# A mixing stage rewritten: four stacked S5 taps, attention in the transposed layout, another order of weights and joins

## The reference, cut to what matters

```python
for l in range(2):
    x = layer_norm(a * x + 0.5 * swiglu(x, ...), ...)      # d_ff 2816
    x = layer_norm(a * x + hybrid_mix(x, ...), ...)
    x = layer_norm(a * x + memory_cross_attention(x, mem, ...), ...)
    x = layer_norm(a * x + 0.5 * swiglu(x, ...), ...)

def hybrid_mix(x):
    dq, dk, dv, mq, mk, mv, mo, mi, mf, su = split_columns(x @ w_in, IN_WIDTHS)
    # differential attention: 4 heads, two maps of width 64 each, values of width 128
    dq, dk = apply_rope(dq), apply_rope(dk)
    s = where(k_chunk <= q_chunk, q k^T / 8, -inf)         # per head and map
    a_out = rms_norm((softmax(s1) - lam * softmax(s2)) @ dv) * (1 - lambda_init)
    # mLSTM: 4 heads of width 64, a causal convolution of 4 taps and silu ahead of it
    mq, mk = silu(causal_conv([mq, mk]))
    h = mlstm_chunkwise(q, k, v, ig, log_sigmoid(f))
    b_out = sigmoid(mo) * rms_norm(h)
    # S5: 16 groups of 16 channels, each driving a complex diagonal state of 64
    states = scan(lam_bar, b_bar @ u);  y = gelu(real(c @ states) + d * u)
    c_out = y * sigmoid(y @ glu_w + glu_b)
    return concat([a_out, b_out, c_out]) @ w_out
```

## Time and profile before

| | us |
|---|---|
| runs | 1377.54, 1377.72, 1380.18; median 1377.72 |
| the profiled execution | 1376.7, span 1374.9, mean granted clock 0.959 |
| PE busy | 1264.1 (92%), 6568 products |
| DVE busy | 812.4 (59%) |
| ACT busy | 578.1 (42%) |
| POOL busy | 192.8 (14%) |
| `mix` of layer 0, x turned to last product | 223.4 to 417 |
| `mix` of layer 1, x turned to last product | 912 to 1089 |

### The profile page before, as it was taken

The page is one execution under the profiler, slowest core; times in us unless marked ns, Lnnn a source line. Parts: engine busy times, 40 slices in busy tenths (PEclk is TensorE's granted clock), DMA queues, the critical chain, the costliest instruction groups (busy, mean ns, idle before and its releaser), DMA issues.

```text
span 1374.9 us, 15895 instructions
## 1 busy us (share of the span) xinstructions
PE 1264.1 (92%) x6568; PEld 1068.6 (78%) x6568; DVE 812.4 (59%) x1130; ACT 578.1 (42%) x656; POOL 192.8 (14%) x181
## 2 busy tenths in 40 slices
PE   6999999989669999999999999999875999799997
PEld 5788888878558888888887888888754887688885
DVE  5578556593675556444566785465937736544454
ACT  4444444425433535444443444444263335444441
POOL 1018000372000000000010180003720000000000
PEclk9999999999789999999999999999976999899999
DMA  8655555433024365555547555544211434455551
GB/s 282 236 184 184 184 184 163 144 123 123 31 92 158 128 204 184 184 188 192 192 148 270 186 184 184 184 151 156 92 61 62 139 118 143 152 184 186 190 193 43
DMA packets 155911, 219.52 MB, mean 160 GB/s; under 512 B 6816, under 2 KB 127776, under 8 KB 155840
## 3 DMA queue, kind: packets, MB, share of 16 engines
q1 hardware_dynamic: 152448, 205.61, 44.9%
q0 software_dynamic: 3120, 11.85, 2.4%
q10 hardware_dynamic: 272, 1.05, 0.2%
HBM read 217.44 MB, written 1.05 MB: 159 GB/s over the span
## 4 chain that ended last, share of the span: by engine, by line
PE 65%; issue 16%; DVE 11%; ACT 3%; POOL 2%; DMA 1%; SPq 0%; DVEq 0%; POOLq 0%
PE PS L469 20%; PE PS L470 19%; PE PS L471 19%; DVE WL L1376 3%; ACT WH L1043 1%; PE PS L500 1%; DMA RAW<-in_ffn_w_up 1%; DVE COUT L1560 1%; DVE ZS L1548 1%; PE PS L964 1%; PE PS L988 1%; ACT XH L1043 1%; PE PS L537 1%; POOL RO L1997 1%; ACT PR L1160 1%
## 5 line engine op out<-in xcount | busy, mean ns | idle before, releaser
L1376 DVE TENSOR_TENSOR WL<-RAW,WH 128x2048 fp32r<-128x2048 f32 (+1 forms) x198 | 445.3, 2253 | 272.4 <-ACT WH L1043 272.3
L1043 ACT ACTIVATE WH<-RAW 128x2048 fp32r<-128x2048 f32 (+1 forms) x198 | 370.5, 1877 | 148.4 <-DMA RAW<-in_ffn_w_up 128.5
L469 PE MATMUL PS<-WH,XH 128*128 128x512 f32 x832 | 333.4, 401 | 24.6 <-DVE WL L1376 9.4
L470 PE MATMUL PS<-WL,XH 128*128 128x512 f32 x832 | 327.5, 394 | 0.0
L471 PE MATMUL PS<-WH,XL 128*128 128x512 f32 x832 | 327.0, 393 | 0.0
L469 PEld LDWEIGHTS PS<-WH,XH 128*128 128x128 f32 x832 | 158.2, 190 | 59.0 <-DVE WL L1376 9.9
L471 PEld LDWEIGHTS PS<-WH,XL 128*128 128x128 f32 x832 | 158.2, 190 | 33.8
L470 PEld LDWEIGHTS PS<-WL,XH 128*128 128x128 f32 x832 | 158.4, 190 | 31.0
L469 PE MATMUL PS<-WH,HH 128*128 128x512 f32 x352 | 138.6, 394 | 5.7 <-issue 5.7
L470 PE MATMUL PS<-WL,HH 128*128 128x512 f32 x352 | 137.6, 391 | 0.0
L471 PE MATMUL PS<-WH,HL 128*128 128x512 f32 x352 | 137.6, 391 | 0.0
(11 more groups left out here) (312 smaller groups left out, 1805.5 us busy)
## 6 DMA issues: line engine op xcount, KB each, us to landing
RAW<-in_ffn_w_gate SPq DMA_DIRECT2D x88, 512.0 KB, 3.7
RAW<-in_ffn_w_up SPq DMA_DIRECT2D x88, 512.0 KB, 4.7
RAW<-in_ffn_w_down SPq DMA_DIRECT2D x88, 512.0 KB, 4.3
RAW<-in_w_in SPq DMA_DIRECT2D x44, 512.0 KB, 4.4
RAW<-in_xattn_wkv SPq DMA_DIRECT2D x32, 512.0 KB, 4.1
RAW<-in_xattn_wq SPq DMA_DIRECT2D x16, 512.0 KB, 4.4
RAW<-in_w_out SPq DMA_DIRECT2D x12, 512.0 KB, 4.0
RAW<-in_xattn_wo SPq DMA_DIRECT2D x12, 512.0 KB, 4.0
```

Source lines behind the costliest of these rows:

```text
L469: nc.tensor.matmul(out_ap, sh, mh, start=first, stop=False)
L470: nc.tensor.matmul(out_ap, sh, ml, start=False, stop=False)
L1043: return nc.scalar.activation(dst, src, ACT.Copy)
L1376: return v.tensor_tensor(dst, full, hi.bitcast(F32), ALU.subtract)
```

## The change

Only `mix`, its preparation in FFN0, the order of its weights and the constants are touched. `xattn`, the FFN products and the boundaries' own work are as before.

- S5 goes by four taps (TAPS = 4, 64 steps). `s5_gather` stacks u by taps on the partitions with 16 products by slices of the identity into one bank, ScalarE copies it to U4. `s5_in` is 16 products with K = 128 and N = 64 (before: 32 with K = 32, N = 128). The states are two batches on VectorE, the turning back included (`s5_states`). `s5_local` is 8 products, `s5_out` 16 with M = 128 (before: 32 with M = 32), `s5_scatter` 16 products that undo the gather, and a copy.
- In FFN0: three `s5_turn` instead of one, `s5_taps` in two parts with N = 128 instead of 64, 12 copies to PB and 8 to KM on ScalarE instead of one and four, `skip_taps` 8 operations instead of 2, one more DMA on GpSimd's queue, KM cleared by GpSimd in each layer.
- DQ and DK are taken in column form, so they come out transposed; `turn_q` and its copies are gone. The rotary turn is on VectorE, in that layout, with TensorE swapping the halves (`swap_halves`, 4 products with N = 512). GpSimd's `rope` and `turn_back` are gone.
- The masks of the diff heads are added by TensorE in PSUM; the maximum and the exponential read PSUM; the row sums come from a column of ones in DV (N = 129), both maps are transposed (6 instead of 3) and multiplied (6 instead of 3), and divided at evacuation.
- Decay: TensorE adds the triangle in `spread`, ScalarE's exponential has the bias; `decay_args` is gone. The first conv tap is on ScalarE, straight from PSUM. Two Newton-like root chains of VectorE are one `pow` each on GpSimd.
- Order: the projections are DV, DQ0, DK0, SU, MQ, MK, DQ1, DK1, MM. The mid units are mid 0, mid 1, W0, W1, mid 2, W2, mid 3, W3, W4. The splits of W3 and W4 stand ahead of the last head, the second join (W3) is taken tile by tile, with the last `turn_cat` between its tiles.

The diff, cut to its core:

```diff
-PAIRS = TILES // 2
-STEPS = SEQ // 2
+BANDS = TILES // 2
+TAPS = 4
+STEPS = SEQ // TAPS
...
-        order += [(l, "DQ", 0), (l, "DQ", 1), (l, "SU", 0), (l, "MQ", 0), (l, "MK", 0), (l, "DK", 0), (l, "DK", 1),
-                  (l, "DV", 0), (l, "DV", 1), (l, "MM", 0), (l, "MM", 1)]
-        order += FILL["mid", l]
-        order += [(l, "W", i) for i in range(5)]
+        order += [(l, "DV", 0), (l, "DV", 1), (l, "DQ", 0), (l, "DK", 0), (l, "SU", 0), (l, "MQ", 0), (l, "MK", 0),
+                  (l, "DQ", 1), (l, "DK", 1), (l, "MM", 0), (l, "MM", 1)]
+        mid = FILL["mid", l]
+        order += mid[0:2] + [(l, "W", 0), (l, "W", 1)] + mid[2:3] + [(l, "W", 2)] + mid[3:4] + [(l, "W", 3), (l, "W", 4)]
...
+            def s5_gather(l):
+                pe.wait_ge(ut_ready.sem, ut_ready.at(l, 1))
+                for tap in range(TAPS):
+                    r = 32 * tap
+                    out_ap = PS[r:r + 32, 5, :].rearrange("p (f j k) -> p j f k", f=2, j=BANDS)
+                    for j in range(BANDS):
+                        mm = nc.tensor.matmul(out_ap[:, j], ident[:, 32 * j:32 * j + 32],
+                                              UT[:, :, tap * STEPS:tap * STEPS + STEPS], start=True, stop=True)
...
+            def diff_scores(l, h):
+                b = head_bank(h)
...
+                for q0, q1, k1 in ((0, P, P), (P, SEQ, SEQ)):
+                    for m in range(2):
+                        r = 64 * m
+                        nc.tensor.matmul(PS[:, b + m, q0:q0 + k1], DQT[r:r + 64, u, h % 2, q0:q1],
+                                         DKT[r:r + 64, u, h % 2, 0:k1], start=True, stop=False,
+                                         skip_group_check=True)
+                        mm = nc.tensor.matmul(PS[:, b + m, q0 + k1 - 64:q0 + k1], kst[r:r + 1, K_EARLY:K_EARLY + P],
+                                              kst[r:r + 1, K_FAR:K_FAR + 64], start=False, stop=True,
+                                              skip_group_check=True)
...
+            def spread(l):
+                pe.wait_ge(cols_read.sem, cols_read.at(l, 1))
+                for i in range(2):
+                    for hh in range(2):
+                        h = 2 * i + hh
+                        pick = ident[0:4, h:h + 1].to_broadcast([4, P])
+                        nc.tensor.matmul(PS[:, i, hh * SEQ:hh * SEQ + SEQ], pick, R_MAX, start=True, stop=False, ...)
+                        nc.tensor.matmul(PS[:, i, hh * SEQ:hh * SEQ + P], ident, tri, start=False, stop=True, ...)
+                        nc.tensor.matmul(PS[:, 3, h * P:h * P + P], pick, R_MAX[:, P:SEQ], start=True, stop=False)
+                        mm = nc.tensor.matmul(PS[:, 3, h * P:h * P + P], ident, tri, start=False, stop=True)
...
+                pe.wait_ge(conv_done.sem, conv_done.at(l, 4))
+                unit_ready(UNIT[l, "MM", 0])
+                form_a_tile(UNIT[l, "MM", 0], 0, 0, XH, XL, 0)
+                swap_halves(l, 3)
+                form_a_tile(UNIT[l, "MM", 0], 0, 0, XH, XL, 1).then_inc(unit_used.sem, 1)
+                diff_scores(l, 1)
+                diff_scores(l, 2)
+                cols(l)
+                s5_scatter(l)
...
+                mid(l, 1, 3)
+                mlstm_scores(l, 0)
+                mlstm_scores(l, 1)
+                diff_out(l, 2)
+                diff_scores(l, 3)
+                mlstm_scores(l, 2)
+                mlstm_scores(l, 3)
+                fill_read("mid", l, 1)
                 mlstm_num(l)
...
                 rows_product(w, [6], CH, CL, True, False)
                 rows_product(w + 1, [7], CH, CL, False, False)
-
+                diff_turn(l, 3)
+                pe.wait_ge(do_read.sem, do_read.at(l, 3))
+                mid(l, 2, 6)
+                diff_out(l, 3)
                 pe.wait_ge(b_ready.sem, b_ready.at(l, 1))
...
+                turn_cat(l, CATM, 0, 7)
+                pe.wait_ge(a_ready.sem, a_ready.at(l, 1))
+                fill_read("mid", l, 2)
+                turn_cat(l, CATA, 0, 6)
...
+                mid(l, 3, 7)
                 pe.wait_ge(cat_lo.sem, cat_lo.at(l, 2))
-                unit_ready(w + 3)
-                rows_tile(w + 3, [0, 1], CH, CL, 0, False, False)
+                unit_ready(w3)
+                rows_tile(w3, [0, 1], CH, CL, 0, False, False)
                 pe.wait_ge(a_ready.sem, a_ready.at(l, 2))
-                turn_cat(l, 2, 2, 5)
+                turn_cat(l, CATA, 2, 4)
```

VectorE's list in the new `mix`, up to the mLSTM:

```diff
+                diff_max(l, 0)
+                s5_states(l, 0)
                 gates_in(l)
+                s5_states(l, 1)
                 split()
                 conv(l, 0)
-                split()
-                s5_turn_in(l, 0)
...
+                mid_split(l, 0)
+                rope(l, 2)
+                gates_out(l)
+                conv(l, 1)
...
+                mid_split(l, 3)
+                diff_sums(l, 2)
+                diff_combine(l, 2)
+                decay_scores(l, 2)
+                decay_scores(l, 3)
```

More of the change, by code:

```diff
@@ L422, in load_ffn, with load_fill @@
                 load_down(l, s, FFN_UNITS - 1, BLOCKS - 1)
-            def load_fill(where, l):
-                for kl, kind, i in FILL[where, l]:
+            def load_fill(where, l, first=0, last=None):
+                for kl, kind, i in FILL[where, l][first:last]:
                     load_cols(UNIT[kl, kind, i], wkv_v, kl, 256 * i + (D if kind == "V" else 0))
@@ L577, in ffn @@
                     rows_product(b + 4 + 3 * j, [0, 1], HH, HL, False, False)
[L578 to L581 removed]
+                    if s == 0 and 5 <= j <= 7:
+                        s5_turn(l, j - 5)
+                    if s == 0 and j == 8:
+                        s5_taps(l, 0)
                 j = BLOCKS - 2
@@ L694, in s5_local, with s5_in @@
+            def s5_in(l):
+                pe.wait_ge(u4_ready.sem, u4_ready.at(l, 1))
+                for i in range(TILES):
+                    for part in range(2):
+                        o = part * 256 + (i % 4) * STEPS
+                        mm = nc.tensor.matmul(PS[:, 4 + i // 4, o:o + STEPS], PB[:, i, part, :], U4[:, i, :],
+                                              start=True, stop=True)
+                    if i % 4 == 3:
+                        mm.then_inc(bu_done.sem, 1)
             def s5_local(l):
@@ new lines, in s5_scatter @@
+            def s5_scatter(l):
+                pe.wait_ge(gelu_done.sem, gelu_done.at(l, 1))
+                g = U4[:, :, :].rearrange("p (f j) k -> p j f k", f=2)
+                for j in range(BANDS):
+                    out_ap = PS[32 * j:32 * j + 32, 2, :].rearrange("p (f a k) -> p a f k", f=2, a=TAPS)
+                    for tap in range(TAPS):
+                        mm = nc.tensor.matmul(out_ap[:, tap], ident[:, 32 * tap:32 * tap + 32], g[:, j],
+                                              start=True, stop=True)
+                mm.then_inc(g4_done.sem, 1)
@@ L875, in mix @@
+                form_b_around(UNIT[l, "DK", 1], 5, lambda: swap_halves(l, 2))
                 s5_out(l, 1)
-                form_a(UNIT[l, "MM", 1], 1, 0, XH, XL)
-                s5_out(l, 2)
-                cols(l)
-                pe.wait_ge(proj_read.sem, proj_read.at(l, 4))
-                if FILL["mid", l]:
-                    memory_unit(FILL["mid", l][0], 3)
-                s5_out(l, 3)
-                turn_q(l, 0)
-                spread(l, 0)
-                spread(l, 1)
-                pe.wait_ge(proj_read.sem, proj_read.at(l, 8))
@@ new lines, in conv_tap @@
+            def conv_tap(l, half):
+                key = (l, ("MQ", "MK")[half], 0)
+                act.wait_ge(unit_used.sem, UNIT[key] + 1)
+                if half == 0:
+                    act.wait_ge(bu_done.sem, bu_done.at(l, 2))
+                for f in range(2 * half, 2 * half + 2):
+                    w = P_CW + 4 * f + 3
+                    nc.scalar.activation(COUT[:, f, :], PS[:, half, (f % 2) * SEQ:(f % 2) * SEQ + SEQ], ACT.Identity,
+                                         bias=PAR[:, P_CB + f:P_CB + f + 1], scale=PAR[:, w:w + 1])\
+                        .then_inc(conv_first.sem, 1)
@@ L1195, in boundary, with mid_out, mid_split @@
                     split()
+            def mid_out(l, i, b):
+                if i < len(FILL["mid", l]):
+                    kv_out(FILL["mid", l][i], b)
+            def mid_split(l, i):
+                if i < len(FILL["mid", l]):
+                    split()
             def mix(l):
```

1110 lines of the change are left out of this document (529 added, 581 removed).

## The result

The changed kernel takes 1430.2 us, the median of four runs from 1429.5 to 1431.1, where the kernel before takes 1377.9: a ratio of 1.038, with a 95% interval of 1.036 to 1.039. The forecast was 1377.7 us, between 1361 and 1392. It is 52 us off, and above the range.

A forecast was written before the change was run, and what follows sets the result against it. FFNs were taken as bound by TensorE's products, mixing stages as also holding idle time and slow clock. Layer 0 +5.5, layer 1 -11.9, FFN0 +6.4 summed to 0.0: 1377.7 us, eight in ten within 1361 to 1392.

The forecast's parts named there:

- The walk of the waits: Four engine queues of `mix` stepped through; layer 0 416.2 to 421.7 us, layer 1 401.1 to 389.2.
- the seven stalls: Layer 1 TensorE waits: MM0 2.4, `spread` 2.3, head 2's copy 2.7, `mlstm_num` 1.1, W0 2.0, last head 1.1, CL 6.2 us.
- eight waits named in layer 0: XL 2.1, MM0 3.5, `spread` 2.7, `mlstm_num` 6.7, W0 2.0, last head's copy 1.5, mid 2's bank 7.7, CL 1.0 us.
- The rival that gave VectorE the bound: VectorE late ahead of MM0, `spread`, `mlstm_num`: +15.5 us, 1393 us; chance .25 together with slow clock.
- The stretched row of before: VectorE's three conv taps: 1.52 us alone, 3.19 while GpSimd turned back for 3.25; forecast not to return.
- The term of the row changes: Diff heads: eight row-count changes at .1 us, no overlap, four masks at .08; 2.4 us a head, +6.4 in four heads.
- The row of before, .33 against .22 us: Product starts 252.27 to 252.60, next step .22; taken to show that a row-count change has a price.
- The step that failed: Clock rule in the `mix` walk: half clock for 4.5 us behind idle stretches over 2.3 us; 9.0 us in layer 0.
- The rival on the clock: Stalls of 1.9 us and more bring half clock: +11.3 us, 1389 us; chance .25 together with VectorE late.
- the gain case: Small products cheaper (1.3 us a head, `spread` 4.4), clock holds through stalls under 2.8 us: 1363.4 us; chance .32.
- FFN0's part: `s5_taps` 1.3 to 3.6 us, two more `s5_turn` .9, no idle time to take them: +3.2 a layer, +6.4.

The follow-up runs named there:

- the one shown: Half of the MK product put between `s5_in` and the gates' turn, against the 1353.1 us kernel (K = 64 masks, sorted `spread`, moved splits and `gates_out`): 1355.9 us.

## Why the prediction was wrong

- **The walk of the waits was right.** Idle time of TensorE was forecast as 27.4 us in layer 0; the trace has 25.9. For layer 1 the prediction gives 27.0 with the slow clock; less its 2.25 us behind each of three stalls of over 2.3 us that is 20.2, and the trace has 20.1 (the seven stalls that it names there add up to 17.8, the same seven in the trace to 17.9). Each of the eight waits named in layer 0 is there within 1.2 us: `mlstm_num` 6.8 (6.7), mid 2's bank 6.6 (7.7), MM0 2.7 (3.5), `spread` 2.8 (2.7); in layer 1 CL is 6.0 (6.2). Moving the splits took 14.7 and 18.5 us away, as that reading implies.
- **The rival that gave VectorE the bound was wrong.** VectorE's conv taps took 2.93 us for six, .49 each, no longer stretched, and it was busy for 110 of 232 us in layer 0. The page SBUF — State Buffer of the Trainium skill, on the shared port pair, says that one of the two engines waits for the whole instruction of the other; GpSimd does nothing beside the taps now, and the .49 us agrees with that. But the taps now read PSUM as well, and no run tells the two apart. The stretched row of before was also paired with the wrong row of GpSimd: the 3.25 us of the earlier trace rows end at 272.16, before the taps start at 272.35. The rest of GpSimd's turning back, until 275.25, is what ran beside them.
- **The term of the row changes was mis-sized.** The prediction took eight changes at .1 us and no overlap: 2.4 us a head. It is 3.5 at full clock; with 1.15 for the same products without a change, .3 a change with the lost overlap in it. The page TensorEngine Tiling (Array Packing) of the Trainium skill says that a change of tiling mode drains TensorE. A price at each change agrees with that; that it is a drain no run here shows. The row of before, .33 against .22 us, held a single change and gave too small a price. `spread` was priced 5.2 and is 7.5 at full clock. `s5_gather` and `s5_scatter`, at 2.4 us each at full clock, were .6 cheaper than forecast. Together the product time at full clock grew by 16.0 and 16.4 us in the layers, not by 14.2 (the terms as listed add up to 14.4): 4 us of the 52.
- **The step that failed is the clock.** "Half clock for 4.5 us behind an idle stretch of over 2.3 us" gave 9.0 and 6.8 us lost; the traces have 28.4 and 29.8. Of the 52 us missed that is 42.4 (19.4 + 23.0), the part that decides it. The rule was read from a trace in which every fall had idle time ahead, and that did not hold for after: the clock fell inside unbroken work, at heads 1 and 2 in both layers. Nor was it back within 4.5 us where small products followed a wait: 17.5 us after the wait ahead of `spread` in layer 0 (351.8 to 369.3), 22.6 after the one of 3.2 us in layer 1 (1084.0 to 1106.6, short waits within). The trace of before had one such stretch, which the rule passed over: 1010.8 to 1024.4 in layer 1, behind 1.9 us of idle time, with small products and more waits in it. With the masks at K = 64 and `spread` sorted the loss is 14.7 and 16.1 us, so about half of it came with the row changes.
- **The rival on the clock was counted too low**, at 1389 us, since it had only shorter idle stretches as its trigger. And the gain case rested on the same short products overlapping: with K = 64 masks they do, 1.15 us a head for the 1.3 that was written there.
- FFN0's part, +3.1 and +3.0 us for +3.2, fits, copies and GpSimd's longer chain hidden as said; no run takes it alone. The rest of the kernel was taken at nothing and is 3.5 us longer: the time lost to half clock there is 6.6 us instead of 2.7, behind waits that were there before.

## What to carry to other kernels

Count the changes of K (the rows of the array in use) in a string of TensorE products before counting the products; a tiny product with another K between two others costs more than the work it does, and here a string of them cost the clock as well. Sort such products by K, or widen the small ones to the K of their neighbours: 64 rows of mask cost less here than one. And when a price of slow clock is read from a trace, note what kind of work came with it, for it holds only for that. A place where the clock falls in one execution and not in another wants a count over many traces before a cause is named.

## What the runs showed of the hardware

- A change of the row count between float32 products costs .20 us (15 changes in `spread` against one: 7.5 and 4.7 us), and takes away the overlap of products on different rows of the array (1.15 us a head without a change, 1.45 with two, 3.5 with eight).
- TensorE's granted clock fell from 2.4 to 1.2 GHz without an idle moment: at heads 1 and 2 in eight of eight stretches with eight changes of the row count a head, in none of eighteen with two or none.
- The same in `spread`: unsorted (339.7 us) in the one trace of it without idle time ahead, sorted in three of five (337.1 in the one shown). So the changes are not the only thing that brings it down.
- A start flag seems to mark the whole bank, not only the columns that its product writes. With the flag on a later product of the bank the outputs were off by a relative error of .23 (sorted `spread`) and .26 (masks behind the scores); with the flag on the first product only, sorted `spread` was right. That products then replace instead of adding is the reading of it.
